# Running sums spread in fp32 instead of bf16 pieces, and one slab of the scan's filler work moved

## The reference, cut to what matters

```python
proj = n @ w_in                       # z, xbc, dt, sc_b, sc_c, sc_x side by side
xbc  = silu(causal_dwconv(xbc, conv_ssd_w) + conv_ssd_b)      # -> xs, Bm, Cm
a    = softplus(dt_raw + dt_bias) * -exp(a_log)               # per head and token
a_cs = cumsum(a)                                              # within a chunk of 128
decay_in = exp(a_cs[i] - a_cs[j])  for i >= j, else 0         # 128 x 128 for every head
y_diag = einsum(cb, decay_in, x_dt);  y_off = einsum(C, prev_states, exp(a_cs))
y    = (y_diag + y_off + d_skip * xs) * silu(z);  y_ssd = rmsnorm per group
y_sc = sc_b * causal_dwconv(sc_c * sc_x, conv_sc_w)
out  = concat(y_ssd, y_sc) @ w_out
```

## Time and profile before

| | |
|---|---|
| median of three runs | 1758.67 us |
| the profiled execution | 1759.0 us, span 1757.3 us |
| mean granted clock of PE | 0.99 |
| PE busy | 1684.9 us (96%) |
| PE weight loads busy | 1516.9 us (86%) |
| DVE busy | 1292.4 us (74%) |
| ACT busy | 1035.1 us (59%) |
| POOL busy | 123.2 us (7%) |
| DMA | 316.64 MB, mean 180 GB/s |

### The profile page before, as it was taken

One profiled execution on the slowest core, in us unless ns is written; L12 is line 12 of the kernel. 1 busy time (PEld: TensorE's weight loads), 2 busy tenths in 40 slices (PEclk: granted clock), 3 DMA queues, 4 the chain that ended last, 5 costly groups with the idle time before them and its releaser, 6 DMA issues.

```text
span 1757.3 us, 34403 instructions
## 1 busy us (share of the span) xinstructions
PE 1684.9 (96%) x10856; PEld 1516.9 (86%) x10856; DVE 1292.4 (74%) x2338; ACT 1035.1 (59%) x1615; POOL 123.2 (7%) x105
## 2 busy tenths in 40 slices
PE   7999999999999999999999999898999998899997
PEld 6998879999999999978888888887778887778886
DVE  5875574699977777767777777787676777877776
ACT  6756554676656666644455555754475666666665
POOL 0014300344410000000000000000000000000000
PEclk9999999999999999999999999999999999999999
DMA  5543256567675555567787777542345554246563
GB/s 190 167 144 98 84 180 215 163 214 210 210 235 176 176 170 176 178 214 242 241 274 243 240 240 242 171 133 84 108 157 193 188 186 153 85 136 203 188 190 109
DMA packets 114411, 316.64 MB, mean 180 GB/s; under 512 B 12752, under 2 KB 45904, under 8 KB 113840
## 3 DMA queue, kind: packets, MB, share of 16 engines
q1 hardware_dynamic: 113504, 311.88, 55.1%
q0 software_dynamic: 848, 4.00, 0.7%
HBM read 296.95 MB, written 18.87 MB: 180 GB/s over the span
## 4 chain that ended last, share of the span: by engine, by line
PE 80%; DVE 10%; ACT 5%; issue 3%; POOL 1%; DMA 0%; ACTq 0%; DVEq 0%; SPq 0%
PE bank L310 10%; PE bank L311 10%; PE bank L312 10%; PE bank L260 9%; PE bank L282 9%; PE bank L261 9%; PE bank L262 9%; PE bank L286 5%; PE bank L1323 3%; DVE wlo L244 2%; ACT whi L236 1%; DVE arena L2044 1%; POOL wlo L1622 1%; DVE arena L1489 1%; DVE arena L1444 1%
## 5 line engine op out<-in xcount | busy, mean ns | idle before, releaser
L244 DVE TENSOR_TENSOR wlo<-raw,whi 128x1024 fp32r<-128x1024 f32 x495 | 609.4, 1233 | 160.5 <-ACT whi L236 150.2
L236 ACT ACTIVATE whi<-raw 128x1024 fp32r<-128x1024 f32 x524 | 550.5, 1052 | 32.3 <-PE bank L304 22.0
L260 PE MATMUL bank<-x,whi 128*128 128x256 f32 (+1 forms) x1728 | 508.4, 294 | 11.6 <-DVE wlo L244 4.0
L262 PE MATMUL bank<-x,wlo 128*128 128x256 f32 (+1 forms) x1728 | 491.9, 285 | 0.0
L261 PE MATMUL bank<-x,whi 128*128 128x256 f32 (+1 forms) x1728 | 491.5, 284 | 0.0
L260 PEld LDWEIGHTS bank<-x,whi 128*128 128x128 f32 x1728 | 331.7, 192 | 17.6 <-issue 12.6
L261 PEld LDWEIGHTS bank<-x,whi 128*128 128x128 f32 x1728 | 332.2, 192 | 0.1
L262 PEld LDWEIGHTS bank<-x,wlo 128*128 128x128 f32 x1728 | 331.3, 192 | 0.0
L310 PE MATMUL bank<-whi,yhi 128*128 128x512 f32 x816 | 321.1, 393 | 8.4 <-DVE ylo L2236 3.0
L311 PE MATMUL bank<-wlo,yhi 128*128 128x512 f32 x816 | 319.7, 392 | 0.0
L312 PE MATMUL bank<-whi,ylo 128*128 128x512 f32 x816 | 319.2, 391 | 0.0
(11 more groups left out here) (316 smaller groups left out, 1744.7 us busy)
## 6 DMA issues: line engine op xcount, KB each, us to landing
raw<-in_stream SPq DMA_DIRECT2D x524, 512.0 KB, 3.5
act_spill<-h SPq DMA_DIRECT2D x128, 128.0 KB, 3.3
h<-act_spill SPq DMA_DIRECT2D x128, 128.0 KB, 3.3
h<-in_x SPq DMA_DIRECT2D x1, 1024.0 KB, 5.1
arena<-in_keys POOLq DMA_DIRECT2D x1, 1024.0 KB, 6.2
h_spill<-h SPq DMA_DIRECT2D x1, 1024.0 KB, 7.6
arena<-h_spill POOLq DMA_DIRECT2D x1, 1024.0 KB, 6.7
arena<-in_g_final POOLq DMA_DIRECT2D x1, 512.0 KB, 8.7
```

The lines of the kernel that those rows point to most:

```text
L236: nc.scalar.activation(whi[:, q * 1024:(q + 1) * 1024], raw[:, q * 1024:(q + 1) * 1024], ACT.Copy).then_inc(hi_ready, 1)
L244: nc.vector.tensor_tensor(wlo[:, q * 1024:(q + 1) * 1024], raw[:, q * 1024:(q + 1) * 1024], whi[:, q * 1024:(q + 1) * 1024].bitcast(F32), ...
L260: nc.tensor.matmul(bank[b][:, 0:T], whi[:, w], xhi[:, x], start=k == 0, stop=False)
L262: last = nc.tensor.matmul(bank[b][:, 0:T], wlo[:, w], xhi[:, x], start=False, stop=k == KT - 1)
```

## The change

It does the following.

- R is made from the fp32 sums themselves: `ident[a, hd:hd + 1]`, a column of the identity on 24 partitions repeated 128 times, times `ACS` (24 x 128). `R3`, `X3`, `SELR`, `SEL3`, the spreading product and the six DVE steps behind it are gone.
- The differences are made by DVE (`decay_differences`) as min(R - own sum, 0), and LL is exp of that without the sign. ACT has EE and LL left. DVE makes those of half k + 1 ahead of the products of half k.
- The order of the slabs is sc0, sc1, sc2, z0 to z11, sc3 to sc11. Each z slab stands one place later; z11 stands behind R of halves 0 and 1 and CB, ahead of the loop. The numbers in `stored`, `X_Z` and the places of the splits follow.

```diff
@@ constants @@
-SC_FIRST = 2
-N_Z = N_SC + SC_FIRST
+N_Z = N_SC + 3
@@ tables of dve_ssd, pe_ssd @@
-        X_Z = {1: 4, 3: 5, 4: 6, 6: 7, 8: 8}
-        K_SC = {-1: 2, 0: 3, 2: 4, 4: 5, 6: 6, 7: 7, 9: 8, 11: 9, 13: 10}
+        X_Z = {1: 3, 3: 4, 4: 5, 6: 6, 8: 7}
+        K_SC = {0: 3, 2: 4, 4: 5, 6: 6, 7: 7, 9: 8, 11: 9, 13: 10}
@@ dve_in_proj @@
-            for r in range(3):
-                nc.vector.tensor_copy(SEL3[32 * r:32 * r + 32, :],
-                                      ident[32 * r:32 * r + 32, 32 * r:32 * r + HEADS]).then_inc(s("sel"), 1)
-            nc.vector.tensor_copy(SELR[0:HEADS, :].rearrange("p (r h) -> p r h", r=3),
-                                  ident[0:HEADS, 0:32].unsqueeze(1).to_broadcast([HEADS, 3, 32])).then_inc(s("sel"), 1)
@@ dve_ssd @@
+            sc_dve(dve, chain, 2)
             split_lo(dve, N_Z + AHEAD, 0, 0, 4)
-            split_lo(dve, N_Z + 1 + AHEAD, 0, 0, 4)
-
-            dve.wait_ge(s("acs_rep"), 1)
-            nc.vector.tensor_copy(X3[0:96, :], bank[5][0:96, 0:SEQ]).then_inc(s("acs_parts"), 1)
...
-            nc.vector.tensor_copy(X3[64:96, :], R3[64:96, :]).then_inc(s("acs_parts"), 1)
+
+            def decay_differences(k):
+
+                c, g, hh = 1 + k // 8, (k // 2) % 4, k % 2
+                dve.wait_ge(s("ee"), k + 1)
+                for x in range(3):
+                    hd = g * GH + hh * 3 + x
+                    nc.vector.tensor_scalar(
+                        DD[:, (k % 2) * 384 + x * P:(k % 2) * 384 + (x + 1) * P],
+                        bank[2 + k % 2][:, x * P:(x + 1) * P],
+                        tok(AC_TOK[c], c)[:, hd:hd + 1], 0.0, ALU.subtract, ALU.min).then_inc(s("dd"), 1)
...
+            decay_differences(0)
             for k in range(4 * GROUPS):
                 m, hh = k // 2, k % 2
+                if k + 1 < 4 * GROUPS:
+                    decay_differences(k + 1)
@@ act_ssd @@
             nc.scalar.activation(DTA[a, 0:1], V("a_log")[a, :], ACT.Exp).then_inc(s("dt_ln"), 1)
+            sc_act(act, 2)
...
-                if k >= 2:
-                    act.wait_ge(s("ll"), k - 1)
-                c, g, hh = 1 + k // 8, (k // 2) % 4, k % 2
-                for x in range(3):
-                    hd = g * GH + hh * 3 + x
-                    nc.scalar.activation(DD[:, (k % 2) * 384 + x * P:(k % 2) * 384 + (x + 1) * P],
-                                         bank[2 + k % 2][:, x * P:(x + 1) * P], ACT.Relu, scale=-1.0,
-                                         bias=tok(AC_TOK[c], c)[:, hd:hd + 1]).then_inc(s("dd"), 1)
...
-                nc.scalar.activation(LL[:, q], DD[:, q], ACT.Exp, scale=-1.0).then_inc(s("ll"), 1)
+                nc.scalar.activation(LL[:, q], DD[:, q], ACT.Exp).then_inc(s("ll"), 1)
@@ pe_ssd @@
-            for m in range(SC_FIRST):
+            for m in range(3):
                 sc_pe(pe, m)
             z_pe(pe, 0)
-            z_pe(pe, 1)
-            pe.wait_ge(s("sel"), 4)
-            pe.wait_ge(s("acs"), 1)
-            nc.tensor.matmul(bank[5][0:96, 0:SEQ], SELR[a, :], ACS[a, META:TM], start=True, stop=True)\
-                .then_inc(s("acs_rep"), 1)
             pe.wait_ge(s("dst"), 2)
...
                     last = nc.tensor.matmul(bank[2 + k % 2][:, x * P:(x + 1) * P],
-                                            SEL3[0:96, hd:hd + 1].to_broadcast([96, P]),
-                                            X3[0:96, (c - 1) * P:c * P], start=True, stop=True)
+                                            ident[a, hd:hd + 1].to_broadcast([HEADS, P]), ACS[a, CHUNK[c]],
+                                            start=True, stop=True)
...
-            z_pe(pe, 11)
-            pe.wait_ge(s("acs_parts"), 5)
+            z_pe(pe, 10)
             half_r(0)
             half_r(1)
             cb(0)
-            sc_pe(pe, K_SC[-1])
+            z_pe(pe, 11)
```

More of the change, by code:

```diff
@@ L214, in stored @@
         def stored(n):
-            if N_SC <= n < N_SC + SC_FIRST:
+            if N_SC <= n < N_SC + 3:
                 return n + XS_T
-            return n - SC_FIRST if N_Z <= n < N_Z + XS_T else n
+            return n - 3 if N_Z <= n < N_Z + XS_T else n
         def load(sp, n0, i, r, U):
@@ L661, in sc_slab @@
         def sc_slab(m):
-            return N_SC + m + (XS_T if m >= SC_FIRST else 0)
+            return N_SC + m + (XS_T if m >= 3 else 0)
         def sc_pe(pe, m):
@@ L809, in dve_ssd @@
                                     ALU.mult).then_inc(s("acs"), 1)
+            sc_dve(dve, chain, 2)
             split_lo(dve, N_Z + AHEAD, 0, 0, 4)
-            split_lo(dve, N_Z + 1 + AHEAD, 0, 0, 4)
-            dve.wait_ge(s("acs_rep"), 1)
-            nc.vector.tensor_copy(X3[0:96, :], bank[5][0:96, 0:SEQ]).then_inc(s("acs_parts"), 1)
-            dve.wait_ge(s("acs_parts"), 1)
-            nc.vector.tensor_tensor(R3[0:96, :], bank[5][0:96, 0:SEQ], X3[0:96, :], ALU.subtract)\
-                .then_inc(s("acs_parts"), 1)
-            dve.wait_ge(s("acs_parts"), 2)
-            nc.vector.tensor_copy(X3[32:64, :], R3[32:64, :]).then_inc(s("acs_parts"), 1)
-            chain.link(nc.vector.tensor_copy(X3[64:96, :], R3[64:96, :]))
-            nc.vector.tensor_tensor(R3[64:96, :], R3[64:96, :], X3[64:96, :], ALU.subtract)\
-                .then_inc(s("acs_parts"), 1)
-            dve.wait_ge(s("acs_parts"), 4)
-            nc.vector.tensor_copy(X3[64:96, :], R3[64:96, :]).then_inc(s("acs_parts"), 1)
             dve.wait_ge(s("tok_tr"), 1)
@@ L832, in dve_ssd @@
             dve.wait_ge(s("tok"), 7)
+            split_lo(dve, N_Z + 1 + AHEAD, 0, 0, 4)
             split_lo(dve, N_Z + 2 + AHEAD, 0, 0, 4)
-            split_lo(dve, N_Z + 3 + AHEAD, 0, 0, 4)
             for j in range(9):
@@ L846, in dve_ssd @@
                     split_lo(dve, N_Z + X_Z[j] + AHEAD, 0, 0, 4)
-            split_lo(dve, N_Z + 9 + AHEAD, 0, 0, 4)
+            split_lo(dve, N_Z + 8 + AHEAD, 0, 0, 4)
             for g in range(GROUPS):
@@ L915, in act_ssd @@
                 z_act(act, j)
-                if j == 2:
+                if j == 1:
                     for c in (0, 1):
@@ L920, in act_ssd @@
                                              ACT.Copy).then_inc(s("btok"), 1)
-                if j == 9:
+                if j == 8:
                     for g in range(GROUPS):
@@ L985, in pe_ssd @@
                              start=True, stop=True).then_inc(s("elb_mm"), 1)
-            z_pe(pe, 2)
+            z_pe(pe, 1)
             pe.wait_ge(s("elb"), 1)
@@ L992, in pe_ssd @@
                 last.then_inc(s("b_tr"), 1)
-            z_pe(pe, 3)
-            pe.wait_ge(s("acs_parts"), 2)
+            z_pe(pe, 2)
             for j in range(9):
@@ L1004, in pe_ssd @@
                     z_pe(pe, X_Z[j])
-            z_pe(pe, 9)
+            z_pe(pe, 8)
             pe.wait_ge(s("btok"), 2)
@@ L1011, in pe_ssd @@
                 if c:
-                    z_pe(pe, 10)
+                    z_pe(pe, 9)
                 for g in range(GROUPS):
```

7 lines of the change are left out of this document (2 added, 5 removed).

## The result

Five runs of the changed kernel took 1768.38 to 1777.15 us, median 1772.97. Five runs of the kernel before took 1755.83 to 1759.0, median 1758.17. The ratio is 1.0085, 95% interval [1.0073, 1.0097]: slower by 0.85%, as forecast in sign. But it is 6 us more than the 1767.0 of the prediction, and outside its range of 1762.5 to 1771.5.

The account below looks back on a forecast made before the run. The prediction took PE, the matmul engine, as the bound. Its terms -1.8 - 1.6 + 3.3 + 1.6 + 7.8 - 1.0 gave +8.3 us on 1759.0, so 1767.3, stated as 1767.0, range 1762.5 to 1771.5.

Parts of the forecast that it names:

- The wait at the first pass: Start of the fifth slab: PE waits 0.35 instead of 2.07 us, -1.8 us; the clock held behind it, -1.6 us.
- The wait at the entry: Loop entry after z11: PE stands still for Silu, Exp table, EE and three differences, +3.3 us (3.0 to 3.5).
- the R products at +7.8: R in the 16 halves: six fp32 records of 0.11 us, 0.66 a half, +0.49 each, +7.8 us in all.
- its own upper bound of 10.7: R products at 0.14 us a record, from later products with a broadcast weight column: +10.7 us.
- my far lower bound: R products at the pace of the seven 24-row transposes, 0.054 us a record: 0.32 a half, +2.4 us.
- the rival that rested on them: R on PE runs as cheaply as the 24-row transposes: +2.4 instead of +7.8, 1761.6 us, not slower; chance 0.10.
- The clock at the entry: Behind the entry wait PE's clock falls to 0.50 during R of half 2 and sc3: +1.6 us (0 to 1.6).
- The end of the loop: ACT, relieved of the differences, delivers the split earlier, so y of half 15 waits less: -1.0 us (0 to -1.5).
- The differences on DVE: In the loop DVE gets 48 operations, about 0.85 us a half or 13.6 us; it fits, with little room.
- The rival of DVE as the bound: MM comes late in seven halves with no slab ahead, PE waits some 0.6 us in each: +4, 1771; chance 0.11.
- the clock holds at the entry: Rival: the entry wait is there but no stretch at 0.50 follows, 1765.4 us; chance 0.15.
- the first pass gains no clock: Rival: PE's clock falls at the first pass as before, +1.6, 1768.6 us; chance 0.06.

Follow-up runs that it names:

- Experiment 2: The kernel before with the new slab order alone (bf16 R, differences on ACT): 1758.74 us, ratio 1.0004.
- Experiment 5: The changed kernel with z11 ahead of R of halves 0 and 1 again and sc3 as the slab ahead of the loop: 1768.47 us, ratio 1.006.
- experiment 6: The changed kernel with 28 unread matmuls of 256 columns behind z11 to fill PE's wait: 1767.96 us, ratio 1.0053.
- experiment 11: The changed kernel with R made over 128 rows, zero beyond the 24: 1770.26 us, ratio 1.0064.
- experiment 10: The changed kernel with nine groups of eight unread fp32 products or transposes behind the last filler slab: 1790.48 us in one run.
- experiment 9: The changed kernel with R in bf16 pieces as before, keeping the new slab order and the differences on DVE: 1761.38 us, ratio 1.0013.
- Experiment 3: The kernel before with the differences on DVE alone: 1758.36 us, ratio 0.9998.
- experiments 1 to 3: The kernel before with one part each: fp32 R alone 1768.39 us, slab order alone 1758.74 us, differences on DVE alone 1758.36 us.

## Why the prediction was wrong

Its direction held, and so did its mechanisms but for that of the loop's end; the size did not.

- *The wait at the first pass* went as written: fifth slab at 101.68 without the late start, against 101.75. Clock 1.00 behind it. -3.5 for -3.4. Experiment 2 shows the same.
- *The wait at the entry* held: 3.18 us for 3.3, by the predicted chain. Experiment 5 confirms its place, and experiment 6 that the clock stays up when PE works through the wait.
- *The step that failed: the R products at +7.8.* The term was mis-sized. In the profile it is +10.4, just inside its own upper bound of 10.7, which had been worked out from the later products with a repeated column. The price of a record, 0.11, was right: inside a row it is 0.112, so 0.67 for the six records of a half (0.66 forecast). What the prediction put at nothing, without a reason, is the edges of a group, that is the two places where R follows and precedes other operations. The first record behind another operation takes up to 0.21, 0.10 more. The last one takes 0.20 to CB, 0.09 more, which experiment 11 takes away. 0.67 + 0.10 + 0.09 is the measured 0.86; ahead of a slab or of y the first record takes 0.18, which makes 0.83. The bf16 R that went was 0.15 to 0.18 ahead of CB and slabs, as I had it, and 0.26 ahead of y. CB's two records in 0.20 are a product between others, which hides its edges. The 24-row transposes of the earlier trace rows, my far lower bound, said nothing on products with two records; the rival that rested on them is refuted.
- *The clock at the entry*, +2.7 for +1.6: the stretch came, as expected, but lasted about 6 us instead of 3.3. I priced it by the one stretch of the earlier trace rows and gave 1.6 as the most that it could cost, while its length is not fixed: with the same code it cost 1.6 in the execution of experiment 10, and 1.5 with bf16 R (experiment 9).
- *The end of the loop*, 0 for -1.0. The chain starts no earlier, because the delay passes from ACT to DVE. DVE at the end of the loop in the changed kernel:

```profile
207.37 1.22 DVE L243 TENSOR_TENSOR wlo<-raw,whi 128x1024 fp32r<-128x1024 f32 x1
208.50 0.43 DVE L689 TENSOR_TENSOR arena<-bank,arena 128x272 f32<-128x272 f32 x1
...
211.12 0.55 DVE L877 TENSOR_TENSOR arena<-arena 128x384 f32<-128x384 f32 x1
```

  DVE stands idle nowhere here. ACT has delivered the split in time, but the last MM (211.12) still stands behind a split and the convolution. Experiment 3 shows the same 1.5 us with this part alone. The prediction counted ACT's relief and left out the differences that stand in DVE's own queue.
- *The differences on DVE* cost nothing in the loop, as written (three in 0.86 us, 0.85 forecast). The rival of DVE as the bound is refuted: PE has no wait on MM inside the loop. That the clock holds at the entry, and that the first pass gains no clock, are refuted too.
- *Not foreseen:* +1.55 us of half rate behind the chunk states and +0.9 at the start. The start differs between all executions (-0.9 to +0.9 against the first). The half rate behind the chunk states came in 7 of the 14 profiled executions of this case, with bf16 and with fp32 R, in either order. It came in both profiles of the changed kernel and not in the one of before that I had read. What decides it is open.

The profiled shift is 7.5 us more than forecast. Of these 2.6 are thus R, 0.5 CB and the slabs around it, 1.1 the clock at the entry, 1.0 the loop's end, and 2.5 stretches of the same code that were slower in this execution; two small terms came out 0.1 below the forecast each. In the medians the miss is 6.0.

The parts alone add up to +0.45% (experiments 1 to 3) where the whole is +0.85%. The traces show less of a gap. From the fourth slab on and without the stretches behind the chunk states, they give 10.7 (R, behind the first pass), 1.1 (the order) and 0.3 (the differences), 12.1 together, where the whole has 13.3, and 1.1 of the difference is the longer half rate at the entry. So no interaction of the parts is shown. What makes the timed gap is open; that the whole change falls into half-rate stretches more often than its parts would fit, but nothing here tests it.

## What to carry to other kernels

Price a group of small fp32 products by the distance of records inside a long row of them, at its own clock, and add the edge in front and the edge behind (here 0.10 and 0.09 us on 0.67); a lone product between others shows neither. When a filler slab changes place, ask what the activation that empties it stands in front of: here a slab with the old function table, placed behind the loop's first products, gave back at the entry what it gained earlier. And a difference of a few us between two profiled executions is only explained when the starts of the same operations are laid side by side, since stretches at half clock come and go by themselves.

## What the runs showed of the hardware

- An fp32 product shows as two records, 0.112 us apart inside a row of them, for 24 or 128 rows (experiment 10); the bf16 products with 96 rows follow each other at 0.057. The Trainium skill ("TensorE: Matmul & The Clock Gate", "Weight-path perf modes — Fast Weight Load (FWL) and DoubleRow") gives fast weight loading to operands of 128 columns that are not fp32. The two paces agree with it, but no run here takes the load apart from the product.
- Where the next operation has another number of rows or of stationary columns, the record before it takes longer. From 24 rows to 128 it cost 0.09 us ahead of an fp32 product and 0.17 ahead of a slab (experiment 11 against the changed kernel), and from 128 columns to 64 and back 0.09 (experiment 10). Padding R to 128 rows gained nothing ahead of y, where the columns change anyway.
- An fp32 transpose of a repeated column is one record where the product is two: three of them ahead of CB took 0.38 us against 0.86 for the products.
- How long PE stayed at 1.2 GHz behind the same wait varied from execution to execution. Behind 3.18 us it was to about 6 us after the wait in both profiles of the changed kernel, and under 4 us in that of experiment 10, whose code is the same up to there. Half rate cost 2.7 us in the one and 1.6 in the other.
